# Two pairs of token blocks in the inverse of the gated delta rule, with block scaling as one operation each

## What is computed

```python
def gated_delta_rule(q, k, v, g, beta):      # float32, chunks of 64 tokens
    gc = cumsum(g)                                            # in each chunk
    decay = exp(where(causal, gc[:, None] - gc[None, :], -inf))
    a = where(strict, (k * beta) @ k.T * decay, 0.0)
    t_inv = inverse(a + eye)                                  # unit lower triangular
    u = t_inv @ (v * beta)
    w = t_inv @ (k * beta * exp(gc))
    intra = where(causal, q @ k.T * decay, 0.0)
    for chunk in chunks:                                      # a scan
        v_new = u - w @ S
        o = (q * exp(gc)) @ S + intra @ v_new
        S = S * exp(gc[-1]) + (k * exp(gc[-1] - gc)).T @ v_new
```

## Time and profile before

| | us |
|---|---|
| median of 3 runs | 1854.47 (1851.41 to 1855.57) |
| the profiled execution, its own time | 1854.16 |
| its span in the trace | 1852.4 |
| from the first M to the first output unit | 1657.4 to 1789.7, 132.3 |
| PE busy over the span | 1792.7 (97%) |
| DVE, ACT busy over the span | 1500.4 (81%), 721.3 (39%) |

### The profile page before, as it was taken

One profiled execution on the slowest core, in us unless ns is written; L12 is line 12 of the kernel. 1 busy time (PEld: TensorE's weight loads), 2 busy tenths in 40 slices (PEclk: granted clock), 3 DMA queues, 4 the chain that ended last, 5 costly groups with the idle time before them and its releaser, 6 DMA issues.

```text
span 1852.4 us, 28952 instructions
## 1 busy us (share of the span) xinstructions
PE 1792.7 (97%) x10379; PEld 1566.0 (85%) x10379; DVE 1500.4 (81%) x2496; ACT 721.3 (39%) x1166; POOL 1048.3 (57%) x653
## 2 busy tenths in 40 slices
PE   7999999999999999999999999999999999999986
PEld 5788879999999999999888888888888686787765
DVE  5786899879998888888489999999999796655544
ACT  3454233333333444344333333333333434325652
POOL 1442355788888555555567777676775463336013
PEclk9999999999999999999999999999999999999998
DMA  9551524899999699899899999999997232210011
GB/s 373 202 172 57 185 77 137 280 318 318 327 319 312 233 305 320 296 309 318 326 339 360 362 356 363 349 363 357 368 353 273 69 92 79 69 57 2 2 57 57
DMA packets 159933, 440.48 MB, mean 238 GB/s; under 512 B 13664, under 2 KB 62944, under 8 KB 156768
## 3 DMA queue, kind: packets, MB, share of 16 engines
q1 hardware_dynamic: 64416, 254.71, 39.7%
q0 software_dynamic: 36864, 134.23, 19.3%
q10 hardware_dynamic: 58560, 50.34, 8.3%
HBM read 386.80 MB, written 52.43 MB: 237 GB/s over the span
## 4 chain that ended last, share of the span: by engine, by line
PE 88%; DVE 6%; DMA 2%; ACT 2%; issue 1%; SPq 0%; ACTq 0%; DVEq 0%
PE PS L974 15%; PE PS L983 15%; PE PS L975 15%; PE PS L1272 9%; PE PS L1273 9%; PE PS L1281 9%; PE PS L1239 4%; PE PS L1317 2%; PE PS L1001 1%; DMA arena<-in_w_ada 1%; PE PS L1308 1%; DVE arena L1946 1%; PE PS L1459 1%; PE PS L1452 1%; DMA gates_d<-arena 1%
## 5 line engine op out<-in xcount | busy, mean ns | idle before, releaser
L862 POOL TENSOR_TENSOR w_lo<-raw,w_hi 128x1024 fp32r<-128x1024 f32 x299 | 720.0, 2409 | 693.2 <-ACT w_hi L1502 692.2
L1502 ACT ACTIVATE w_hi<-raw 128x1024 fp32r<-128x1024 f32 x332 | 352.1, 1060 | 923.3 <-PE PS L983 570.7
L974 PE MATMUL PS<-act_hi,w_hi 128*128 128x384 f32 (+1 forms) x1584 | 576.4, 364 | 2.2 <-DVE act_lo L1914 0.7
L975 PE MATMUL PS<-act_lo,w_hi 128*128 128x384 f32 (+1 forms) x1584 | 562.8, 355 | 0.0
L983 PE MATMUL PS<-act_hi,w_lo 128*128 128x384 f32 (+1 forms) x1584 | 337.2, 354 | 0.0
L974 PEld LDWEIGHTS PS<-act_hi,w_hi 128*128 128x128 f32 x1584 | 299.0, 189 | 34.9 <-DVE act_lo L2379 4.9
L975 PEld LDWEIGHTS PS<-act_lo,w_hi 128*128 128x128 f32 x1584 | 299.1, 189 | 23.3 <-issue 2.6
L1272 PE MATMUL PS<-w_hi,act_hi 128*128 128x512 f32 x768 | 300.4, 391 | 3.4 <-ACT arena L1658 3.4
L983 PEld LDWEIGHTS PS<-act_hi,w_lo 128*128 128x128 f32 x1584 | 284.5, 188 | 22.6 <-issue 0.5
L1273 PE MATMUL PS<-w_hi,act_lo 128*128 128x512 f32 x768 | 300.2, 391 | 0.0
L2326 DVE TENSOR_TENSOR act_lo<-arena,act_hi 128x384 fp32r<-128x384 f32 x128 | 249.1, 1946 | 29.6 <-ACT act_hi L1716 29.6
(11 more groups left out here) (358 smaller groups left out, 1913.2 us busy)
## 6 DMA issues: line engine op xcount, KB each, us to landing
raw<-in_expert_u SPq DMA_DIRECT2D x128, 512.0 KB, 5.4
raw<-in_expert_v SPq DMA_DIRECT2D x128, 512.0 KB, 5.9
raw<-in_w_in SPq DMA_DIRECT2D x52, 512.0 KB, 3.7
arena<-in_w_ada SPq DMA_DIRECT2D x24, 1024.0 KB, 9.6
gel_d<-arena ACTq DMA_DIRECT2D x64, 384.0 KB
gates_d<-arena ACTq DMA_DIRECT2D x12, 2048.0 KB, 15.4
arena<-gates_d SPq DMA_DIRECT2D x32, 768.0 KB, 7.0
arena<-gel_d SPq DMA_DIRECT2D x32, 768.0 KB, 8.8
```

The lines of the kernel that those rows point to most:

```text
L862: pool.tensor_tensor(w_lo[:, k % SPLIT, :], raw[:, k % RAW, :], w_hi[:, k % SPLIT, :].bitcast(F32), ALU.subtract).then_inc(lo_split, 1)
L974: pe.matmul(own, w, act_hi[:, c, 0:n_tok], start=(i == 0), stop=False)
L975: pe.matmul(own, w, act_lo[:, c, 0:n_tok], start=False, stop=False)
L1502: act.activation(w_hi[:, k % SPLIT, :], raw[:, k % RAW, :], ACT.Copy).then_inc(hi_split, 1)
```

## The change

The list of steps is written anew, and three things are done with other instructions. Level 0 stays for all four token blocks. Then `invert_two(0, ...)` takes blocks 0 and 1 through levels 1 to 6, with one attention step after each of their 12 products M, and `invert_two(2, ...)` takes blocks 2 and 3, with tokens, solve, read, scan and gsquare of the first two blocks between. Solve, read and scan of blocks 2 and 3 follow, with attention steps 25 to 32 among them. Attention steps per level of one token block, and all products, are as many as before.

The column scaling of a token block is three DVE operations of 128x512 with the column broadcast along the row, where there were eight on the DVE (128x128 each) and four on ACT. The sums of squares of the first three blocks are one DVE multiplication and one DVE reduction, where they were four ACT operations. The scan's new values get four places of their own.

```diff
     steps += [("unit", 28), ("mask", 0, 0), ("mask", 0, 1), ("unit", 29)]
     fill = 30
-    for level in range(LEVELS):
-        for what, tb in (("M", 0), ("M", 1), ("X", 0), ("M", 2), ("X", 1), ("M", 3), ("X", 2), ("X", 3)):
-            if (what, level) == ("X", 0):
-                steps.append((what, level, tb))
-            if what == "X":
-                if fill < 32:
-                    steps.append(("unit", fill))
-                elif fill == 33:
-                    steps += [("values", q) for q in range(TB)]
-                    attend()
-                elif fill > 33 and not (level == 6 and tb % 2):
-                    attend()
-                fill += 1
-            if (what, level) != ("X", 0):
-                steps.append((what, level, tb))
-            if (what, level, tb) in (("X", 5, 1), ("X", 6, 1)):
-
-                steps.append(("tokens", level - 5))
-            if what == "M" and 4 * level + tb + 2 < 4 * (LEVELS - 1):
-                steps.append(("mask", level + (tb + 2) // 4, (tb + 2) % 4))
-
-    for kind, n in (("solve", 0), ("tokens", 2), ("solve", 1), ("read", 0), ("scan", 0), ("tokens", 3), ("solve", 2),
-                    ("read", 1), ("scan", 1), ("solve", 3), ("read", 2), ("scan", 2), ("read", 3), ("scan", 3)):
+    masks = iter([(0, 2), (0, 3)] + [(level, pair + tb) for pair in (0, 2) for level in range(1, LEVELS - 1) for tb in (0, 1)])
+
+    def product(level, tb):
+
+        steps.append(("M", level, tb))
+        if level < LEVELS - 1:
+            steps.extend(("mask", *at) for at in itertools.islice(masks, 1))
+
+    for what, tb in (("M", 0), ("M", 1), ("X", 0), ("M", 2), ("X", 1), ("M", 3), ("X", 2), ("X", 3)):
+        if what == "M":
+            product(0, tb)
+        else:
+            steps.append(("X", 0, tb))
+            if tb < 2:
+                steps.append(("unit", 30 + tb))
+    steps += [("values", q) for q in range(TB)]
+    attend()
+
+    def invert_two(tb, between):
+
+        for level in range(1, LEVELS):
+            product(level, tb)
+            if level > 1:
+                steps.append(("X", level - 1, tb + 1))
+            steps.extend(between.get((level, 0), ()))
+            attend()
+            steps.append(("X", level, tb))
+            product(level, tb + 1)
+            steps.extend(between.get((level, 1), ()))
+            attend()
+        steps.append(("X", LEVELS - 1, tb + 1))
+
+    invert_two(0, {(5, 0): [("tokens", 0)], (6, 0): [("tokens", 1)]})
+    invert_two(2, {(1, 0): [("solve", 0)], (2, 0): [("read", 0), ("scan", 0), ("gsquare", 0)], (3, 0): [("solve", 1)],
+                   (3, 1): [("read", 1)], (4, 1): [("scan", 1), ("gsquare", 1)], (5, 0): [("tokens", 2)],
+                   (6, 0): [("tokens", 3)]})
+    for kind, n, count in (("solve", 2, 1), ("read", 2, 1), ("solve", 3, 0), ("scan", 2, 2), ("read", 3, 2), ("scan", 3, 2)):
         steps.append((kind, n))
         if kind == "scan":
             steps.append(("gsquare", n))
             if n == 3:
                 steps.append(("groot", 1))
-        if kind in ("tokens", "read", "scan"):
...
@@ -1807,16 +1841,9 @@
                     act.activation(AO[:, 0, :], AO[:, 0, :], ACT.Exp).then_inc(dt_ready, 1)
                 if kind == "M" and n:
                     wait_full(act, "m", n, tb)
-                    act.wait_ge(d_ready, 4 * n + tb + 3)
+                    act.wait_ge(d_ready, x_done(*same_buffer_before(X_STEPS, n, tb)))
                     own = slice(0, P) if n < LEVELS - 1 else HI
                     act.activation(M1[own, tb % 2, 0:256], PS[own, bank("m", n, tb), 0:256], ACT.Copy).then_inc(m1_ready, 1)
-                if kind == "tokens":
-                    wait_full(act, "kt", tb)
-                    act.wait_ge(tok_dve, tb + 1)
-                    for h in range(GH):
-                        ins = act.activation(cv[:, 4 + h, t], PS[:, bank("kt", tb), h * P:(h + 1) * P], ACT.Copy,
-                                             scale=egcum[:, 32 + 4 * tb + h:33 + 4 * tb + h])
-                    ins.then_inc(tok_act, 1)
                 if kind == "solve":
                     wait_full(act, "wt", tb)
                     act.activation(Dm[:, tb, :], PS[:, bank("wt", tb), :], ACT.Copy)
@@ -1830,23 +1857,16 @@
                     if tb == 0:
                         act.wait_ge(*lowered(U_OUT2 - 1))
                     act.activation(avt[:, tb, :], PS[:, bank("av", tb), :], ACT.Copy).then_inc(avt_ready, 1)
-                if kind == "gsquare":
-                    if n == 0:
-                        act.wait_ge(bank_full[JOBS[("o", 0)] % 4], JOBS[("o", 0)] // 4 + 1)
-                    if n < TB - 1:
-                        act.wait_ge(o_ready, n + 1)
+                if kind == "gsquare" and n == TB - 1:
+                    act.wait_ge(gsq_ready, n)
+                    wait_full(act, "o", n)
                     for h in range(GH):
-                        if n:
-                            act.wait_ge(gsq_ready, 4 * (n - 1) + h + 1)
-                        if n == TB - 1 and h == 0:
-                            wait_full(act, "o", n)
-                        src = otok[:, h, t] if n < TB - 1 else PS[:, bank("o", n), h * P:(h + 1) * P]
-                        act.activation(gscratch[:, h, :], src, ACT.Square,
+                        act.activation(gscratch[:, h, :], PS[:, bank("o", n), h * P:(h + 1) * P], ACT.Square,
                                        accum_out=gsum[:, 4 * n + h:4 * n + h + 1]).then_inc(gsq_ready, 1)
                 if kind == "groot":
 
                     own = slice(0, 12) if n == 0 else slice(12, 16)
-                    act.wait_ge(gsq_ready, own.stop)
+                    act.wait_ge(gsq_ready, TB - 1 + 4 * n)
                     act.activation(grms[:, own], gsum[:, own], ACT.Sqrt, bias=eps, scale=1.0 / P).then_inc(g_root, 1)
                 if kind == "logits":
...
@@ -2551,11 +2571,19 @@
                         dve.wait_ge(*lowered(U_OUT2 + 1))
                     if tb >= 2:
                         wait_full(dve, "u", tb - 2)
-                    per_head(KB[:, tb % 2, :], ("kt", tb), bge, 4 * tb)
-                    per_head(VB[:, tb % 2, :], ("vt", tb), beta, 4 * tb, last=tok_dve)
+                    def by_head(col4):
+                        return col4.unsqueeze(2).to_broadcast([P, GH, P])
+
+                    own, kt = slice(4 * tb, 4 * tb + 4), h4(PS[:, bank("kt", tb), :])
+                    wait_full(dve, "kt", tb)
+                    v.tensor_tensor(h4(KB[:, tb % 2, :]), kt, by_head(bge[:, own]), ALU.mult)
+                    wait_full(dve, "vt", tb)
+                    v.tensor_tensor(h4(VB[:, tb % 2, :]), h4(PS[:, bank("vt", tb), :]), by_head(beta[:, own]),
+                                    ALU.mult).then_inc(tok_dve, 1)
+                    v.tensor_tensor(cv[:, 4:8, t], kt, by_head(egcum[:, 32 + 4 * tb:36 + 4 * tb]), ALU.mult).then_inc(kd_ready, 1)
                 if kind == "read" and tb:
                     wait_full(dve, "ws", tb)
-                    v.tensor_tensor(M1[:, tb % 2, :], AT[:, tb, :], PS[:, bank("ws", tb), :], ALU.subtract).then_inc(vn_ready, 1)
+                    v.tensor_tensor(new_values(tb), AT[:, tb, :], PS[:, bank("ws", tb), :], ALU.subtract).then_inc(vn_ready, 1)
                 if kind == "scan":
...
@@ -2571,6 +2599,10 @@
                                                              in1=PS[:, bank("su", tb), h * P:(h + 1) * P],
                                                              op0=ALU.mult, op1=ALU.add)
                             ins.then_inc(state_ready, 1)
+                if kind == "gsquare" and n < TB - 1:
+                    dve.wait_ge(o_ready, n + 1)
+                    chain.link(v.tensor_tensor(gscratch[:, :, :], otok[:, :, t], otok[:, :, t], ALU.mult))
+                    v.tensor_reduce(gsum[:, 4 * n:4 * n + 4], gscratch[:, :, :], AX_X, ALU.add).then_inc(gsq_ready, 1)
                 if kind == "groot":
                     own = slice(0, 12) if n == 0 else slice(12, 16)
                     dve.wait_ge(g_root, n + 1)
```

39 lines of the change are left out of this document (26 added, 13 removed).

## The result

The changed kernel takes 1862.76 us (median of 16 runs, 1856.82 to 1865.93) where the kernel before, on the same chip, took 1855.05 (1850.73 to 1857.53). The ratio is 1.0043, with a 95% interval of 1.0035 to 1.0052, which is 8.0 us more (6.5 to 9.6). The forecast of 1859.0 stood 4.0 above that median (and 4.8 above the profiled execution of before, 1854.16). The direction was right, and the size is half of what came.

The account below looks back on a forecast made before the run. The prediction took PE as the bound, busy 118.9 of 132.3 us in the changed stretch. From 1854.2 us, 8.9 removed, 10.7 of new waits and 3.0 of half clock gave 1859.0, range 1847.5 to 1863.

Parts of the forecast that it names:

- waits of 1725 to 1757 and at `pv` 7, gone: PE's waits where levels 5 and 6 end and tokens and solve begin, 4.4 us, and at `pv` 7, 0.95, removed.
- new waits: PE waits added by the new list, from the start to item 27's `turn`, 10.7 us in all.
- tail, last `both_logits` to last `pv`: End of the attention steps: 13.6 to 14.6 us where 15.9 before, a gain taken as 1.7.
- half clock around 1730, gone: Products slowed after 1.6 us of idle time from 1728.6 to 1731.2 return to full clock, 1.8 us removed.
- half clock behind new waits: Slow clock after the long waits of steps 11 and 28, 3.0 us added, bounds 0 and 5.
- Step 11: Attention step 11: level 5's X and three scalings delay the gate's product on the DVE; PE waits 2.5 us.
- Steps 27 and 28: Block 2's state update and gsquare precede the gate's product on the DVE; PE waits 3.0 and 0.6, 3.6 us.
- The table loads: Two added ACT_TABLE_LOADs, behind the second root and ahead of the last: one hidden, one 0.15 us late but absorbed.
- Mostly hidden: Rival, 17%: of the new waits only the start's 0.5 and some 1.5 stay and the clock holds; 1847 us.
- exchange: Rival, 23%: half of the added waits, 5.4 us, and one slow spell, 1.8; 1852.5 us.
- DVE heavier: Rival, 5%: scalings of 3 us and a reduction of 1.1 lengthen several steps, with more half clock; 1864.7 us.
- What would show it: Signs: waits of about 3 us at step 28 and 1.6 at step 11, scalings 0.69 each, half clock after both.

Follow-up runs that it names:

- b2: The changed kernel with the sums of squares of blocks 0 to 2 back on ACT; 1858.09 us, ratio 1.0018 to the kernel before.
- d4: The changed kernel with sums of squares back on ACT and idle products in three of PE's waits; 1855.61 us, ratio 1.0008 to the kernel before.
- a2: The changed kernel with the list of steps of before, keeping the new scalings and sums of squares; 1851.31 us, ratio 0.9983 to the kernel before.
- a4: The changed kernel with products nobody reads in PE's waits at steps 12, 24 and 28; 1857.58 us, ratio 1.0013 to the kernel before.

## Why the prediction was right in direction and short in size

Term by term, in the order of its sum:

| term | forecast | measured |
|---|---|---|
| waits of 1725 to 1757 and at `pv` 7, gone | -5.35 | in the old form gone |
| new waits | +10.7 | +10.3 |
| tail, last `both_logits` to last `pv` | -1.7 | -2.1 (13.8 for 15.9) |
| half clock around 1730, gone | -1.8 | gone; its size is from the one profile of before |
| half clock behind new waits | +3.0 | +7, what is left of +8.0 |

**The waits** are right nearly one by one. Start 0.5: from M to `both_logits` 64 products take 3.12 us (1676.17 to 1679.29) where 80 took 3.12 before (1676.57 to 1679.69), so the time of 16 products, 0.5, is now wait. Step 11 2.5: 1.53 + 0.44 + 0.52 = 2.49. Steps 15 and 16 0.6: 0.31, gone in b2 with the gsquare. Steps 19 to 21 1.45: 1.42. Steps 22 to 24 1.6: 0.68 + 0.99 = 1.67. Steps 27 and 28 3.6: 2.77 + 0.58 = 3.35. Item 27's `turn` 0.45: 0.56. Sum 10.3. That was worked out by walking down the queues of DVE and ACT from one known event, with starts from one item to the next, and the estimates for the operations not seen before (0.61 for a scaling, 0.65 for the reduction) met 0.60 and 0.60.

**The tail** was forecast as 13.6 to 14.6 and took 13.8. Its own idle time rose, from 5.3 (2.54, 0.39, 0.31, 0.58, 0.78, 0.69) to 6.1 us (2.53, 0.54, 1.57, 0.78, 0.69); the gain is the full clock in it. At half clock, as in b2, it takes 15.4, a gain of 0.5. So most of the 1.7 was a clock gain and not a shorter chain, and I had not told them apart: this term is right by its sum, in part by luck. (The `read` that the 15.9 leaves out took 1.06 by its starts and not 0.9, so the gain is nearer 1.9.)

**The clock is the step that failed.** I put "about the 1.8" to each of the two longest waits and took 3.0 for half clock behind the new waits, with 5 as the upper bound. What is left of the measured 8.0 after the other terms (-5.35 + 10.3 - 2.1 - 1.8 = 1.05) is 7 us. Two other readings come near it. The profiled executions of the changed kernel have 9.4 us of half-clock time in the stretch in the mean; their mean granted clock is 0.9875, and that of all 24 runs 0.9860, which is another 5.6, and half of 15.0 is 7.5. (That takes all of the 5.6 to lie in this stretch, which the 24 runs don't say, and half is the most that it can cost.) And the idle products at three places gave back 5.6 (3 to 8); in d4, with shorter waits, only 1.9. Where it lies is seen in the four profiles: at four places and not two, with X of level 6 (0.99, and 0.68 and 1.42 ahead of it) among them, and up to 6.8 us at one place. The first X is one that both orders share (its half clock shows in a2 too), so not all of it is the change's. What I had was one execution: the 0.95 at `pv` 7 came through at full clock, and I let no wait of that size cost anything, nor several of them close together. That holds at `pv` 7 in all profiles of the old order, but not at X of level 6, where three waits stand within 12 us.

The same seen from the whole execution: from a mean of 110 to a mean of 24 runs the time rises by 8.4 us, and the idle time of PE by 5.9 and half of the half-clock time, its upper price, by 2.6 (47.1 to 52.3) make 8.5. In the forecast the waits made +5.35 and all the clock terms together, the tail's among them, -1.8 - 1.7 + 3.0 = -0.5. So the waits were right here too, and the clock some 3 us short, all that the forecast lacks. The gain that I booked for the lost spells at 1730 and in the tail, 10.2 us of half clock in the one profile, has been more than eaten up by new ones.

**The table loads** cost nothing, as forecast. That the one behind the roots hides was seen (1.6 us of room). The one ahead of the last root shows in no time either: from the first output unit to the end of the span 62.7 us pass in both kernels (1789.7 to 1852.4 and 1792.8 to 1855.5). **The rivals.** "Mostly hidden" and "exchange" fall with the waits, all of which stand in the profile. "DVE heavier" would have been 1864.7, near what came, but its mechanism is not there: scalings at 0.60 and not 0.8 or more. Its last two us, more half clock, were the part of it that happened. **What would show it**: all held, apart from the clock, which in the first profile was low behind step 28 only.

What stays open: the size of the clock term is a remainder, 5.5 to 8.6 by the interval of the result, and rests on single profiles for the other terms; of the direct measures a4's says no more than that it is above 3 in the changed kernel. Nor is it known what decides whether a wait is followed by half clock in one execution and not in another. The split of the 7 us among the places is known from four executions only. Of the 4.6 us that the sums of squares cost on the DVE, 1.6 are not found in the waits.

## What to carry to other kernels

A new order of steps is priced by walking the queues of the engines beside PE down to PE's next hard wait; done item by item this came out within 0.5 us in 10. The clock behind the waits needs a price of its own, from several executions and not from one in which some of the waits went unpunished. A few products that nobody reads, put into the waits, measure it, but here with an interval of some 2.5 us to either side, and the half clock can turn up at a later wait instead. Half of the half-clock time is an upper bound of what it costs, for where PE waits anyway slower products use up the wait. Take an operation's and an order's effects apart before judging a change: here two of its parts had opposite signs, and the operation that showed no cost in one order (the sums of squares) cost 4.6 us in the other.

## What the runs showed of the hardware that was not expected

- The granted clock at the same place, with the same waits to 0.01 us, differs from one execution to the next: behind the waits of step 11 (1.53, 0.44 and 0.52) it was 1.00 in two executions and low in two, in one of them so early that `both_logits` took 1.65 us and not 0.92, and the 0.52 was used up.
- Half clock at a place where PE waits anyway cost nothing: in a4 13 products took 2.93 us for 1.64, the wait behind them 0.28 for 1.57, and the stretch 13.8 us as at full clock.
- A DVE reduction of 128x512 to 128x4 takes 0.69 us (0.60 to the next start), and a product with a column broadcast over each head's 128 columns, 128x512, 0.68 (0.60), no more than a plain one. Three of them take 1.9 us, where eight of 128x128, which are two thirds of the same work, took 2.15.
